# Expert loop of a mixture-of-experts decoder trunk: down chunks one block further behind, and the transposes of the hidden block one chunk later

## The reference, cut to what matters

```
for e in range(N_EXPERTS):                       # 8 experts, D_EXPERT = 3584
    out = out + gate[:, e:e+1] * swiglu(t, w_gate[e], w_up[e], w_down[e])
swiglu(u, wg, wu, wd) = (silu(u @ wg) * (u @ wu)) @ wd
```

## Time and profile before

| | |
|---|---|
| median of the three runs | 1778.92 us |
| the profiled execution's own time | 1774.83 us |
| its span | 1773.1 us |
| TensorE matmuls busy | 1634.2 us, 92% |
| VectorE busy | 1319.5 us, 74% |
| ScalarE busy | 1036.2 us, 58% |
| mean granted TensorE clock | 0.955 |

### The profile page before, as it was taken

One profiled execution on the slowest core, in us unless ns is written; L12 is line 12 of the kernel. 1 busy time (PEld: TensorE's weight loads), 2 busy tenths in 40 slices (PEclk: granted clock), 3 DMA queues, 4 the chain that ended last, 5 costly groups with the idle time before them and its releaser, 6 DMA issues.

```text
span 1773.1 us, 21411 instructions
## 1 busy us (share of the span) xinstructions
PE 1634.2 (92%) x8119; PEld 1363.0 (77%) x8119; DVE 1319.5 (74%) x1128; ACT 1036.2 (58%) x846; POOL 14.5 (1%) x35
## 2 busy tenths in 40 slices
PE   5997799998799777999999999999999999999985
PEld 5986688886697766887887887887878878878864
DVE  6975445445697545887888888888888888888874
ACT  4535243434453433776776766767767767767752
POOL 3000000000000000000000000000000000000000
PEclk9997799998899677999999999999999999999998
DMA  9431355553343114998997998998999989989940
GB/s 288 143 120 47 100 168 191 190 172 114 98 140 124 43 47 146 370 369 291 380 366 277 378 371 295 371 349 304 368 344 318 373 326 337 364 312 345 372 176 24
DMA packets 203022, 439.17 MB, mean 248 GB/s; under 512 B 12056, under 2 KB 31072, under 8 KB 202976
## 3 DMA queue, kind: packets, MB, share of 16 engines
q1 hardware_dynamic: 197040, 437.32, 69.2%
q10 hardware_dynamic: 5936, 1.21, 0.4%
HBM read 437.46 MB, written 1.05 MB: 247 GB/s over the span
## 4 chain that ended last, share of the span: by engine, by line
PE 77%; DVE 12%; ACT 5%; issue 5%; ACTq 0%; DVEq 0%; POOL 0%; POOLq 0%
PE bank L1129 23%; PE bank L1130 22%; PE bank L1131 22%; DVE wlo L721 3%; ACT whi L649 3%; PE bank L1199 2%; PE bank L1124 1%; PE bank L1403 1%; DVE uTl L757 1%; PE bank L1257 1%; PE bank L1453 1%; DVE scores L854 1%; DVE work L1059 1%; ACT work L480 1%; DVE work L752 1%
## 5 line engine op out<-in xcount | busy, mean ns | idle before, releaser
L721 DVE TENSOR_TENSOR wlo<-raw,whi 128x2048 fp32r<-128x2048 f32 x415 | 945.9, 2290 | 263.0 <-ACT whi L649 145.7
L649 ACT ACTIVATE whi<-raw 128x2048 fp32r<-128x2048 f32 x341 | 652.4, 1916 | 173.2 <-PE bank L1131 173.2
L1129 PE MATMUL bank<-whi,uTh 128*128 128x512 f32 (+1 forms) x1312 | 524.2, 400 | 19.7 <-DVE uTl L757 17.0
L1130 PE MATMUL bank<-wlo,uTh 128*128 128x512 f32 (+1 forms) x1312 | 512.5, 391 | 0.0
L1131 PE MATMUL bank<-whi,uTl 128*128 128x512 f32 (+1 forms) x1312 | 512.3, 390 | 0.0
L1129 PEld LDWEIGHTS bank<-whi,uTh 128*128 128x128 f32 x1312 | 249.2, 190 | 78.9 <-DVE uTl L757 14.5
L1131 PEld LDWEIGHTS bank<-whi,uTl 128*128 128x128 f32 x1312 | 249.2, 190 | 52.7
L1130 PEld LDWEIGHTS bank<-wlo,uTh 128*128 128x128 f32 x1312 | 249.5, 190 | 50.1 <-issue 1.7
L1129 PE MATMUL bank<-whi,hTr 128*128 128x512 f32 x552 | 218.2, 395 | 8.5 <-DVE hTr L920 5.1
L499 ACT ACTIVATE whi<-raw 128x2048 fp32r<-128x2048 f32 x74 | 141.5, 1912 | 141.1 <-PE bank L1131 139.6
L1130 PE MATMUL bank<-wlo,hTr 128*128 128x512 f32 x552 | 216.7, 393 | 0.0
(11 more groups left out here) (203 smaller groups left out, 1225.3 us busy)
## 6 DMA issues: line engine op xcount, KB each, us to landing
raw<-in_w_exp_gate_dram SPq DMA_DIRECT2D x112, 1024.0 KB, 7.1
raw<-in_w_exp_up_dram SPq DMA_DIRECT2D x112, 1024.0 KB, 6.8
raw<-in_w_exp_down_dram SPq DMA_DIRECT2D x112, 1024.0 KB, 7.0
raw<-in_w_in_dram SPq DMA_DIRECT2D x28, 1024.0 KB, 5.5
raw<-in_w_ffn_gate_dram SPq DMA_DIRECT2D x11, 1024.0 KB, 5.0
raw<-in_w_ffn_up_dram SPq DMA_DIRECT2D x11, 1024.0 KB, 4.9
raw<-in_w_ffn_down_dram SPq DMA_DIRECT2D x11, 1024.0 KB, 4.8
raw<-in_w_out_dram SPq DMA_DIRECT2D x8, 1024.0 KB, 5.0
```

The lines of the kernel that those rows point to most:

```text
L649: nc.scalar.activation(whi[:, s % SPLIT, :], raw[:, s % RAW, :], ACT.Copy).then_inc(hi_a, 1)
L721: return V.tensor_tensor(wlo[:, n % SPLIT, :], raw[:, n % RAW, :], whi[:, n % SPLIT, :].bitcast(F32), ALU.subtract).then_inc(lo_ready, 1)
L1129: T.matmul(o, sth, mvh, start=start, stop=False)
L1130: T.matmul(o, sth, mvl, start=False, stop=False)
```

## The change

`EXP_ORDER` puts the two up chunks of block r ahead of the two down chunks of block r-1. The transposes of block r-1 stand behind the second gate half instead of the first, ScalarE's copy of them behind the Silu, and VectorE's part at the first up chunk. The transposed block has two buffers, by the parity of the block. At the end of an item, what was down 5, up 6, down 6 becomes up 6, down 5, down 6: the first gather stands behind the last up chunk as before, then come the first down chunk of block 5, the last transposes and the second gather. `LAST_UP` falls from chunk 39 to chunk 37, and with it `SELECT_AT` from 35 to 33. No operation is added or removed.

```
-    EXP_ORDER += [... (("g", _r), ("d", _r - 1), ("u", _r)) for _h in range(2)]
+    EXP_ORDER += [... (("g", _r), ("u", _r), ("d", _r - 1)) for _h in range(2)]
...
-        exhT = [hTr[:, i, 0:NC].rearrange(...) for i in range(2)]
+        exhT = [[hTr[:, i, j * NC:(j + 1) * NC].rearrange(...) for i in range(2)] for j in range(2)]
...   ScalarE
-                    if kind == "g" and hf == 0 and r >= 1:
-                        turn_hi(i, r - 1)
                     if kind == "g" and hf == 1:
                         act.wait_ge(consumed, i * EXP_LOADS + (NSTATIC + n + 1))
                         nc.scalar.activation(exs[r % 2], bank(r % 2), ACT.Silu).then_inc(exsil, 1)
+                        if r >= 1:
+                            turn_hi(i, r - 1)
...
                     if n == LAST_UP:
                         tokens_hi(i + 1, 0)
-                        turn_hi(i, r)
+                    if n == LAST_UP + 1:
+                        turn_hi(i, EXR - 1)
...
-                    if n == LAST_UP:
+                    if n == LAST_UP + 1:
                         tokens_hi(i + 1, 1)
...   VectorE
-                    if kind == "g" and hf == 0 and r >= 1:
+                    if kind == "u" and hf == 0 and r >= 1:
                         turn_lo(r - 1)
...
                     if n == LAST_UP:
                         tokens(i + 1, 0)
-                        turn_lo(r)
+                    if n == LAST_UP + 1:
+                        turn_lo(EXR - 1)
...
-                    if n == LAST_UP:
+                    if n == LAST_UP + 1:
                         tokens(i + 1, 1)
                         tokens_lo(i + 1)
...   TensorE
-                    if kind == "g" and hf == 0 and r >= 1:
+                    if kind == "g" and hf == 1 and r >= 1:
                         turn(r - 1)
...
                         gather(i + 1, 0)
-                        turn(r)
+                    if n == LAST_UP + 1:
+                        turn(EXR - 1)
                         gather(i + 1, 1)
```

More of the change, by code:

```diff
@@ L71 @@
 for _r in range(1, EXR):
-    EXP_ORDER += [(_k, _c, _h) for _k, _c in (("g", _r), ("d", _r - 1), ("u", _r)) for _h in range(2)]
+    EXP_ORDER += [(_k, _c, _h) for _k, _c in (("g", _r), ("u", _r), ("d", _r - 1)) for _h in range(2)]
 EXP_ORDER += [("d", EXR - 1, 0), ("d", EXR - 1, 1)]
@@ L205, in trunk @@
         uTeh, uTel = uTh[:, :, 0:P], uTl[:, :, 0:P]
-        exhT = [hTr[:, i, 0:NC].rearrange("p (c n) -> p c n", c=4) for i in range(2)]
+        exhT = [[hTr[:, i, j * NC:(j + 1) * NC].rearrange("p (c n) -> p c n", c=4) for i in range(2)] for j in range(2)]
         ye = region(4096, D)
@@ L594, in turn_hi @@
                 act.wait_ge(exT_ps, i * EXR + (r + 1))
-                nc.scalar.activation(exhT[0], bank(4, 4, P), ACT.Copy).then_inc(exT_hi, 1)
+                nc.scalar.activation(exhT[r % 2][0], bank(4, 4, P), ACT.Copy).then_inc(exT_hi, 1)
             norm(0, lambda t: act.wait_ge(x_in, 16), -1)
@@ L1074, in turn_lo @@
                     dve.wait_ge(exT_hi, i * EXR + (r + 1))
-                    V.tensor_tensor(exhT[1], bank(4, 4, P), exhT[0].bitcast(F32), ALU.subtract).then_inc(exT_ready, 1)
+                    V.tensor_tensor(exhT[r % 2][1], bank(4, 4, P), exhT[r % 2][0].bitcast(F32), ALU.subtract).then_inc(exT_ready, 1)
                 for n, (kind, r, hf) in enumerate(EXP_ORDER):
-                    if kind == "g" and hf == 0 and r >= 1:
+                    if kind == "u" and hf == 0 and r >= 1:
                         turn_lo(r - 1)
@@ L1417, in _ @@
                             s = slice(q * NC, (q + 1) * NC)
-                            last = product(bank(5 + q), exhT[0][:, cc, :], exhT[1][:, cc, :], wh[:, c, s], wl[:, c, s],
+                            last = product(bank(5 + q), exhT[r % 2][0][:, cc, :], exhT[r % 2][1][:, cc, :], wh[:, c, s], wl[:, c, s],
                                            start=r == 0 and cc == 0, stop=end and c == 1)
```

## The result

The changed kernel is slower: 1781.91 us, the median of 13 runs (1780.14 to 1785.62), against 1773.72 us for the kernel before, also 13 runs (1771.06 to 1779.92). The ratio is 1.0046, 95% interval 1.0037 to 1.0056: a small loss, but clear of the scatter of the runs. The profiled execution of the changed kernel has a span of 1782.4 us, 9.3 more than before.

A forecast was written before the change was run, and what follows sets the result against it. TensorE bounds the kernel. Terms +1.60 + 0.05 - 0.34 - 0.28 = +1.03 us an item, times 8 = +8.2 on 1774.83 us: 1783.1; half of 4.1 added: 1785; range 1779 to 1790.

The forecast's parts named there:

- The stall in the middle: First down chunk of blocks 0 to 4 gets its weight load late: 5 x 0.32 = +1.60 us an item.
- T: Time at which the transposes of block r-1 start in the new order.
- `select`: Standing two chunks earlier, it no longer makes a split late: -0.34 us an item.
- The end of the item: From G to the third scatter, less two chunks, 13.97 against 14.25 us: -0.28 us an item.
- G: Start of the first gather at the end of an item.
- The sum: All terms together: +1.03 us an item, times 8 = +8.2 us, giving 1783.1 us.
- What could be won at most: TensorE's listed waits and late chunk starts together: 2.63 us an item, 21 us in the kernel.
- A (hidden): Late load in the middle hidden (1770.3 us) or at half price (1776.7 us); chance 0.15.
- B (the stall spreads): A second chunk in each of five blocks also waits about 0.22 us: 1792 us; chance 0.11.
- the split that I held for thin: VectorE's split behind the product, done by T + 11.0, needed for a load at T + 11.1 + 0.3.
- C (clearly faster): All waits at the item's end go, no stall in the middle: -1.28 us an item, 1764.6 us; chance 0.04.
- price bounds: Late loads in five blocks: +0.80 us an item if only the matmul's delay counts, +2.15 if the whole gap.

The follow-up runs named there:

- e1: Changed kernel with VectorE's turn_lo moved ahead of the split behind the second gate half: 127.34 us an item, 1763.83 us, ratio 0.993.
- e4: Changed kernel with turn_lo done twice, the second giving exT_ready: 134.40 us an item (mean of two), 1818.64 us, one time.
- e6: Kernel before with select four chunks earlier, behind chunk 31: 128.24 us an item, 1770.6 us, one time.
- e7: e1 with the next item's second chunk rounded and split behind the copies at the item's end: 125.13 us an item, 1750.68 us, ratio 0.9868.
- e2: Changed kernel with transposes, turn_hi and turn_lo of middle blocks back behind the first gate half: 127.31 us an item, 1769.56 us, one time.
- e8: Kernel before with the next item's second chunk rounded and split behind the end copies: 126.43 us an item, 1763.11 us, ratio 0.9938.
- e5: Kernel before, old chunk order, with transposes and turn_lo behind the second gate half, turn_hi behind the Silu: 149.29 us an item, 1945.48 us.

## Why the prediction was right, point by point

**The stall in the middle** was right in place, count and cause. The first load was worked out for T + 6.07 and came at T + 6.14; five blocks in an item have it, the last two do not; e1 takes it away and e4 lengthens it by just the operation added. Its price was 0.36 us and not 0.32, as the load came 0.07 later: +1.80 us an item instead of +1.60. The step at fault is the one from the end of a VectorE operation to the load that waits for it: the row gave 0.04, the forecast wrote "about 0.1" and used 0.06, and behind `turn_lo` it was 0.13 (from T + 6.01 to T + 6.14). Among the bounds, the one that counts only the matmul's delay (0.16) was wrong here. One sign to look for was wrong: the profile of the changed kernel puts the gap down to "issue", and only e4 shows `turn_lo` by name.

**`select`**: -0.34 worked out, the chunks at that place are 2.72 us long after, and e6 measures -0.35 by itself.

**The end of the item**: -0.28 worked out, -0.34 measured, but with a wrong inside. I expected the wait for L682 to shrink to 0.7 us; it grew to 1.47. The copy itself came when I said (first scatter at G + 16.59, worked out 16.63), but TensorE was there earlier: a gather takes 1.70 us. The 2.05 between 1189.87 and 1191.92 before, which I took for the length of a gather ("over 2 us"), held a wait of the down chunk for its own `turn_lo` (L1075, 1191.10 to 1191.79), which the profile does not list by that name. The sum did not suffer, because VectorE's row of operations sets the third scatter, and not TensorE's. The wait for L1098 doubled from 0.40 to 0.81, as forecast.

**The sum**: +1.80 + 0.07 - 0.34 - 0.34 = +1.19, of which 0.04 is given back at the other late split (it costs 0.19 instead of 0.23; the chunk is the first gate half of block 1, not the first up half as the forecast calls it). That leaves 1.15, where 1.11 was measured and 1.03 worked out; the rest is what adding figures rounded to hundredths leaves. The forecast was 8.2 us, and the medians differ by 8.2. That they agree so closely is luck: the two profiled executions differ by 9.3 us, and the item was worked out 0.08 us too low.

**What could be won at most.** The forecast said 2.63 us an item, and e7 won 3.46. The forecast added up the lengths of the waits that the profile lists, and a wait costs more than its listed length. Around the listed wait of 0.44 us for the product, 2.38 us pass from the first gather to the transposes, where a gather alone needs 1.70. The second gather held 0.35 us more. From the start of the last chunk to the first scatter, with the listed wait of 1.22 us, 4.10 us pass where e7 needs 2.72.

**The rivals.** A (hidden) is out by the gaps, B (the stall spreads) by the gate chunks behind, all 2.72 us: the split that I held for thin, needed for a load at T + 11.4, ended at 1137.00 + 2.29, T + 11.02. C (clearly faster) failed in the changed kernel, but it was closer than its chance of 0.04 says: the order by itself (e2) wins 1.28 us an item, and e1 shows that one line stood in the way. That 1.28 is also C's number is chance: C let the wait for L681 shrink by 0.55, and in e2 it shrank from 1.22 to 0.9. **The median**: half of 4.1 us was added because the three runs shown lay above the profiled execution. Thirteen runs put the kernel before at 1773.72, so nothing should have been added; 1783.1 would have been closer to 1781.91 than 1785. The forecast's own range of 1779 to 1790 is the price bounds and this half of 4.1 alone; the 3 us of scatter that it names are not in it.

## What to carry to other kernels

Where each engine executes a fixed list, ask for each handed-over result not when its operation could run, but what stands ahead of it in its engine's list, and whether the engine is idle just before that: here a 0.7 us operation whose input had been ready for 4 us waited behind a split whose input was not, and swapping the two is worth more than the whole change. Read a kernel that has lost in parts: this one is a gain of 1.28 us and a loss of 2.39 us an item in one diff. Where a TensorE-bound loop has a seam between items, look at which work for the next item stands ahead of the copies that TensorE waits for (e7, e8: 2.2 us an item for moving one chunk).

## What the runs showed of the hardware that was not expected

- A semaphore that comes 0.1 us too late for the matmul costs more than 0.1 us, since the weight load ahead of it is late too. Gaps on PEld of 0.31, 0.47 and 0.47 us cost 0.22, 0.34 and 0.36 us: about the gap less 0.1.
- The whole price of a wait of TensorE is not always its length. The waits of 1.47 us (changed kernel) left the granted clock at 1.00 over the item. Behind 37 of 42 waits of 1.85 to 2.10 us in e5 the clock fell for a part of the next two chunks, which then took 7.2 us instead of 5.6. In e4 one of the waits of 1.84 us was followed by a clock of 0.65 over the scatters, and the others, just as long, were not. So the length of the wait alone does not decide it; what else does is not shown here.
- A gap whose releaser is another engine's semaphore can be listed as "issue" (0.47 us, changed kernel). The 0.35 us inside the second gather before are in no row of the matmuls at all, and the weight load at 1191.92 shows 0.29 of them as "issue".
